# Norms of x turned by a diagonal of reciprocals, and output weights in chunks of 512 by 512

## What is computed

```python
def rmsnorm(x, g):
    xf = x.astype(jnp.float32)
    y = xf * lax.rsqrt(jnp.mean(xf * xf, axis=-1, keepdims=True) + EPS)
    return (y * g.astype(jnp.float32)).astype(x.dtype)
...
        h = rmsnorm(x, norm_mix_g[l])
...
        x = x + merged @ w_o[l]

        h = rmsnorm(x, norm_ffn_g[l])
...
        h = rms_norm(x, norm_mix[i]) * (1 + scale1) + shift1
...
    return o.reshape(B, S, MLA_HEADS * MLA_V) @ w_o
...
        x = x + gate1 * y
        h = rms_norm(x, norm_mlp[i]) * (1 + scale2) + shift2
```

## Time and profile before

| | us |
|---|---|
| median of 3 runs | 1577.72 |
| lowest and highest | 1576.03 and 1578.23 |
| the profiled execution | 1578.04 |
| its span | 1576.2 |
| PE busy | 1530.2 |
| DVE busy | 1151.1 |
| ACT busy | 820.7 |
| POOL busy | 132.2 |

### The profile page before, as it was taken

One profiled execution on the slowest core, in us unless ns is written; L12 is line 12 of the kernel. 1 busy time (PEld: TensorE's weight loads), 2 busy tenths in 40 slices (PEclk: granted clock), 3 DMA queues, 4 the chain that ended last, 5 costly groups with the idle time before them and its releaser, 6 DMA issues. The chain is left out here.

```text
span 1576.2 us, 25674 instructions
## 1 busy us (share of the span) xinstructions
PE 1530.2 (97%) x10406; PEld 1359.2 (86%) x10406; DVE 1151.1 (73%) x1501; ACT 820.7 (52%) x1113; POOL 132.2 (8%) x119
## 2 busy tenths in 40 slices
PE   7999999999999999999998899999999999999998
PEld 6999989999799998999987688887788888878887
DVE  6898678785778767778579667777878766776665
ACT  6464444444646444444478654454556555554442
POOL 2150000000114000000014000000111112000000
PEclk9999999999999999999999999999999999999999
DMA  9766366666676636667632347667886765346652
GB/s 327 266 216 204 131 231 230 212 238 243 234 268 210 209 117 234 207 215 277 235 126 86 101 143 278 243 226 210 266 310 234 269 169 197 108 144 217 207 172 102
DMA packets 229908, 327.45 MB, mean 208 GB/s; under 512 B 12216, under 2 KB 187808, under 8 KB 229792
## 3 DMA queue, kind: packets, MB, share of 16 engines
q1 hardware_dynamic: 222728, 315.11, 59.4%
q10 hardware_dynamic: 7064, 10.71, 1.9%
HBM read 316.32 MB, written 9.47 MB: 207 GB/s over the span
## 5 line engine op out<-in xcount | busy, mean ns | idle before, releaser
L1751 DVE TENSOR_TENSOR wparts<-raw,wparts 128x2048 fp32r<-128x2048 f32 (+1 forms) x240 | 545.6, 2279 | 211.4 <-ACT wparts L1263 211.1
L1263 ACT ACTIVATE wparts<-raw 128x2048 fp32r<-128x2048 f32 (+1 forms) x240 | 454.8, 1898 | 127.8 <-PE bank L563 92.8
L561 PE MATMUL bank<-hT,wparts 128*128 128x256 f32 x1216 | 348.7, 287 | 2.2 <-DVE hT L1852 1.5
L562 PE MATMUL bank<-hT,wparts 128*128 128x256 f32 x1216 | 343.9, 283 | 0.0
L563 PE MATMUL bank<-hT,wparts 128*128 128x256 f32 x1216 | 343.9, 283 | 0.0
L561 PEld LDWEIGHTS bank<-hT,wparts 128*128 128x128 f32 x1216 | 233.0, 192 | 6.8 <-issue 5.6
L562 PEld LDWEIGHTS bank<-hT,wparts 128*128 128x128 f32 x1216 | 233.2, 192 | 0.2
L563 PEld LDWEIGHTS bank<-hT,wparts 128*128 128x128 f32 x1216 | 233.1, 192 | 0.0
L561 PE MATMUL bank<-wparts,aT 128*128 128x512 f32 (+2 forms) x568 | 217.8, 383 | 1.8 <-DVE aT L1916 1.3
L561 PE MATMUL bank<-wparts,hT 128*128 128x512 f32 (+2 forms) x592 | 211.5, 357 | 3.4 <-DVE wparts L1751 1.6
L562 PE MATMUL bank<-wparts,aT 128*128 128x512 f32 (+2 forms) x568 | 213.5, 376 | 0.0
(11 more groups left out here) (287 smaller groups left out, 1890.9 us busy)
## 6 DMA issues: line engine op xcount, KB each, us to landing
raw<-in_mlp_w SPq DMA_DIRECT2D x64, 1024.0 KB, 5.5
ada_raw<-in_ada_w SPq DMA_DIRECT2D x96, 512.0 KB, 6.4
raw<-in_w_ffn_in SPq DMA_DIRECT2D x44, 1024.0 KB, 5.6
raw<-in_w_in SPq DMA_DIRECT2D x43, 1024.0 KB, 5.5
raw<-in_dil_w_in SPq DMA_DIRECT2D x64, 512.0 KB, 4.8
raw<-in_w_ffn_out SPq DMA_DIRECT2D x22, 1024.0 KB, 5.1
raw<-in_w_o SPq DMA_DIRECT2D x8, 1024.0 KB, 4.8
biasb<-head_bias ACTq DMA_DIRECT2D x16, 512.0 KB, 6.1
```

What stands on the lines that cost most here:

```text
L561: pe.matmul(dst, held[:, 0, :], streamed[:, 0, :], start=start, stop=False)
L562: pe.matmul(dst, held[:, 0, :], streamed[:, 1, :], start=False, stop=False)
L1263: act.activation(view(whi[c % SPL], c), view(raw[c % RAW], c), ACT.Copy).then_inc(s_hi, 1)
L1751: dve.tensor_tensor(view(wlo[c % SPL], c), view(raw[c % RAW], c), view(whi[c % SPL], c).bitcast(F32), ALU.subtract).then_inc(s_lo, 1)
```

## The change

**Turning.** x is no longer multiplied. DVE multiplies the 128 x 128 identity by a tile's reciprocals, one to a row, into a diagonal (`turning_diagonal`), once for each token tile, and PE multiplies a block of x by it: the product is the block turned and scaled. That is an ordinary fp32 matmul in place of a transpose. `norm_upper` on ACT and `norm_lower` on DVE are gone; the tiles `xn...` of 128 x 2 x 1024 become `turner...` of 128 x 2 x 128. `TURN_EARLY` is as before.

**Chunks.** `w_o` and the latent output weights come as four chunks of 512 rows by 512 columns. `wide_half` takes two chunks for one half of the output columns, with a bank for each token tile: 24 matmuls of 512 columns a chunk. `four_for_weights` gives the ring of weights a fourth bank for the time. DVE adds four times 512 columns, after the second and the fourth chunk, and ACT squares four times 512 columns where it squared 768 and 256 of each tile. In the latent part, chunk 0 waits for pairs 0 to 3 of the heads, chunk 1 for pairs 4 to 7.

```diff
             for c in range(4):
-                chunk(("WO", l, c), kmajor(A["w_o"][l], 256 * c, 256))
+                out_half, half = divmod(c, 2)
+                chunk(("WO", l, c), kmajor(A["w_o"][l][512 * half:512 * half + 512], 512 * out_half, 512))
...
-            def norm(e, xn):
+            def norm(e, turner):
...
-                    return pe.transpose(banks[k][:, P * t:P * t + P], xn[:, t, P * k:P * k + P], ident[:, :])
-
-                pe.wait_ge(s_xn, 2 * e + 1)
+                    return pe.matmul(banks[k][:, P * t:P * t + P], x[:, t, P * k:P * k + P], turner[:, t, :], start=True, stop=True)
+
+                pe.wait_ge(s_turner, 2 * e + 1)
                 for k in TURN_EARLY[e]:
-                    if k == 4:
-                        pe.wait_ge(s_xn2, 2 * e + 1)
                     turn_block(k, 0)
+                pe.wait_ge(s_turner, 2 * e + 2)
...
+                four_for_weights()
                 for c in range(4):
+                    out_half, half = divmod(c, 2)
                     w = weights(("WO", l, c))
-                    if c < 3:
-                        token_major(("WO", l, c), w, 0, 256, hT, 0, DK, first_of=None if c else ("mg", l))
-                        used(("WO", l, c))
-                for t in range(TT):
-                    token_major(("WO", l, 3, t), w, 0, 256, hT, 0, DK, (t,))
-                used(("WO", l, 3), ("WO", l, 3, 1))
-                norm(2 * l + 1, xnf)
+                    wide_half(("WO", l, out_half), ("WO", l, c), w, half, None if out_half else ("mg", l))
+                three_for_weights()
+                norm(2 * l + 1, turnerf)
...
             def wo():
-                for h in range(0, MH, 2):
-                    emptied(pe, ("OT", unitm(h) // 2))
+                four_for_weights()
                 for c in range(4):
+                    out_half, half = divmod(c, 2)
+                    if c < 2:
+                        for pair in range(4 * half, 4 * half + 4):
+                            emptied(pe, ("OT", unitm(0) // 2 + pair))
                     w = weights(("MO", 0, c))
...
+                    wide_half(("MO", 0, out_half), ("MO", 0, c), w, half, a=aT)
+                three_for_weights()
...
-            def norm_lower(ev, xn, t):
+            def turning_diagonal(ev, turner, t):
                 i = RSTD_OF[ev] + t
                 dve.wait_ge(s_rstd, i + 1)
-                dve.tensor_scalar(xn[:, t, 0:512], x[:, t, 0:512], rstd[:, i % 2, 0:1], None, ALU.mult).then_inc(s_xn, 1)
...
+                dve.tensor_scalar(turner[:, t, :], ident[:, :], rstd[:, i % 2, 0:1], None, ALU.mult)\
+                   .then_inc(s_turner, 1)
...
+                for c in range(3):
+                    split_ahead(("WO", l, c))
+                    if c == 0:
+                        continue
+                    half = c - 1
+                    for t in range(TT):
+                        nm = ("WO", l, half, t)
+                        bk = full(dve, nm)
+                        xs = x[:, t, 512 * half:512 * half + 512]
+                        dve.tensor_tensor(xs, xs, bk[:, :], ALU.add).then_inc(drain_sem(nm), 1)
+                        if (half, t) == (1, 0):
+                            norm_mean(2 * l + 1, 0)
+                norm(2 * l + 1, turnerf)
```

More of the change, by code:

```diff
@@ L592, in _, with wide_half @@
             wide_banks = {}
-            def wide_half(name, chunk_name, w, half, first_of=None, between=idle):
+            def wide_half(name, chunk_name, w, half, first_of=None, between=idle, a=hT):
                 at = 4 * half
@@ L962, in _ @@
             mlp(0)
[L965 removed]
+            norm(6, turnerd)
             four_for_weights()
@@ L1819, in norm @@
                     dve.sem_inc(s_ss, 1)
+                if 0 < ev < 7:
+                    turning_diagonal(ev, turner, 0)
                 norm_mean(ev, 1)
-                if ev in (0, 7):
-                    norm_lower(ev, xn, 0)
-                norm_lower(ev, xn, 1)
+                if ev == 0:
+                    dve.wait_ge(s_const, 16)
+                for t in range(1 if 0 < ev < 7 else 0, TT):
+                    turning_diagonal(ev, turner, t)
             hc, lc = [0], [0]
```

143 lines of the change are left out of this document (45 added, 98 removed).

## The result

| | median | lowest to highest | runs | against before |
|---|---|---|---|---|
| before | 1577.94 | 1575.10 to 1581.27 | 19 | |
| after | 1581.56 | 1577.75 to 1585.75 | 19 | 1.0022 (1.0015 to 1.0028) |

What follows compares the result with a forecast made beforehand. PE, busy for 97% of the span, was taken as the bound, with its idle time at the norms and MO. Terms from +1.5 (norm 0) to -2.65 us (MO) summed to -2.5 on 1578.04: 1575.5 us, range 1573.5 to 1578.5.

Steps and rivals of the forecast that it cites:

- The turning product: Turning one block on PE by an fp32 product with the diagonal: 0.24 us at full clock, 0.45 at half.
- The rival of 0.43 at full clock: A turning product costs as much as a 256-wide one: some 20 us slower in all, 1595 us; chance 0.08.
- The diagonal: DVE makes the diagonal in 0.24 us instead of multiplying x, so each norm's second turning starts 0.25 earlier.
- w_o with norms 1 and 3: Two layers' output weights and following norms: wide chunks -0.9 us, norm +0.43 each; together -0.95.
- Norm 0: First norm, turned at half clock with nothing to hide the products: +1.5 us (1.0 to 1.9).
- Norm 2: Products keep PE busier, so the clock holds and the projection starts earlier: -0.55 us; +1.0 if the clock falls.
- MO: Latent attention's output weights: early start -1.5 us, wide matmuls -1.15; together -2.65.
- Norm 5: Norm behind the latent output: wider DVE and ACT work, but no half-clock stretch; -0.75 us (-0.3 to -1.35).
- Norms 6 and 7: Last two norms, clock undecided by the rows; taken to fall as before: +0.9 us.
- one case: In norms 6 and 7 the clock falls for 3.4 us as it did: +0.8 and +1.2 us.
- The other case: In norms 6 and 7 the clock holds: 0.25 us gained in norm 6, nothing in norm 7.
- clock falls everywhere: Rival: norm 2 costs 1.55 us more, norms 6 and 7 1.1 more; 1578.1 us, no change; chance 0.13.

Runs made afterwards that it cites:

- filled067: The changed kernel plus identity products (overwritten, output unchanged) that keep PE busy ahead of norms 0, 6 and 7; 1575.82 us, 0.9984 of before.
- before_again: The kernel before, unchanged, profiled a second time; 1580.36 us in one execution.
- products_only: The kernel before with all norms turned by products with the diagonal, keeping its own 256-column chunks; 1580.75 us, 1.0009 of before.
- before_held: The kernel before plus products of the identity in front of norms 1 to 7, no other change; 1576.22 us, 0.9985 of before.
- held_transposes: The kernel before with the new chunks, seven table loads later and identity products ahead of norms 1 to 7, still turning by transposes; 1571.51 us, 0.9955 of before.
- held_products: The changed kernel, turning by products, with seven table loads later and identity products ahead of norms 1 to 7; 1576.04 us, 0.9982 of before.
- chunks_only: The changed kernel with all eight norms turned by transposes as before, leaving only the 512 by 512 chunks; 1574.26 us, 0.9977 of before.
- latent_held: The kernel before with 512 by 512 chunks for the latent output weights only, table loads later, identity products ahead of norms 1 to 7; 1572.53 us, 0.9967 of before.
- after_again: The changed kernel, unchanged, profiled a second time; 1582.7 us in one execution.

## Why the prediction was wrong, step by step

- **The turning product, 0.24 at full clock and 0.45 at half: right.** 16 blocks are 32 records; in norm 2 they take 4.25 us with the wait for the second diagonal, in filled067's norm 7 0.12 each. At half clock they stand 0.213 apart, 0.43 a product. The rival of 0.43 at full clock is out.
- **The diagonal, 0.24: 0.28 to 0.29.** It comes 0.2 earlier than the multiplied x did.
- **w_o with norms 1 and 3, -0.95: -0.93 at the first projection (2.24 to 1.76, 2.14 to 1.69), and then given back, +0.7 and +1.1.** The term failed, since it stops at the first projection and left out the loads behind SP's wait for the second half of x, for which PE waits 0.6 and 1.7 us in after. That the edit itself made it worse isn't shown. In after and in before_again alike, PE waits from some 5.6 to 5.8 us between issue and ACT's start on; the loads took 6.36, 7.56, 7.06 and 6.67 us in the two profiles of after, and 5.55, 6.30, 5.85 and 6.65 in those of before.
- **Norm 0, +1.5 (1.0 to 1.9): +2.0 at the first projection, +1.8 after 48 more matmuls: right.** Over five profiles with products and no filling ahead of norm 0 it is +1.3 to +1.8 there. The shift of 2.2 by 154 us is not norm 0's alone: in products_only it shrinks from 1.5 to 0.8 on the same way.
- **Norm 2, -0.55 for a clock that holds: -0.55, which is luck.** The products did hold it, here and in the six other profiles that have products and nothing ahead there. But five of six profiles with transposes and nothing ahead hold it too, by a norm of 15.83 us, and products at full clock are 0.1 slower. What I booked as the change's gain was a fall that before's one profile happened to have.
- **MO, -2.65: -2.70**, of which 1.37 by the early start (1.68 to 0.31 behind the last value product) and 1.33 by the wide matmuls (22.99 to 21.66), where 1.5 and 1.15 were forecast; the two misses cancel. It repeated in every kernel that has it; the second chunk was never late.
- **Norm 5, -0.75: -0.4 in this pair of profiles, inside its range.** As in norm 2, the clock's part of it (before 15.86, 15.09 in its second profile, 14.64 in before_held) isn't the change's.
- **Norms 6 and 7, +0.9 by taking one of two: +1.2 and +2.1, the largest miss.** They fell, as one case had it, at +0.8 and +1.2. That case itself was sized too small: I valued before's start in norm 7 at 1395.5 instead of 1394.72, since its next matmuls ran at half clock. But behind the start PE waits for h anyway, so that the half clock cost before nothing (14.71 fallen, 14.70 held). With products it cost 1.5. The other case was off as well: with the clock held the products don't gain 0.25 in norm 6 and lose nothing in norm 7, they lose 0.05 and 0.5 against transposes with the clock held.

In the traces the forecast is 5.7 us off (-2.5 against +3.2): 2.4 in norms 6 and 7, 1.8 in w_o with norms 1 and 3 and the wait behind them, 0.7 up to the end of the first mixer, 0.3 in MO with norm 5, and 0.5 in norm 4 and the mixers' drift. The state that came, a fall in norms 6 and 7 and none in norms 2 and 5, was worth 1576.6 at the prediction's own prices, so that the clock's choice explains 1 us of the miss and the prices the rest.

What the failed steps on the clock share: I compared the changed kernel's likely clock with one profile's clock of before, and added the difference to medians of many executions. The chances followed from that: 'clock falls everywhere' (1578.1) had 0.13 and was still 3.5 us short of the measured time.

The rule of the Trainium skill that speaks against the edit (Perfetto Trace Analysis, section Transposes: do a logical transpose as a transpose, not as a standard matmul) was the better guide: held_transposes against held_products agrees with it, 1571.51 to 1576.04 us. The Trainium skill's other rule (TensorE: Matmul & The Clock Gate, Part 4: PE-mode transpose), by which transposes don't count as busy for the clock as matmuls do, isn't borne out in before_again's norm 2, where transposes are PE's only work and the granted clock is 1.00. The 9 falls in 30 norms against 1 in 35 go the way of that rule, but a product also keeps PE busy twice as long as a transpose, and no run tells the two apart.

What is not settled: why a load takes 5.2 or 7.6 us; what places a fall of the clock, above all in the latent heads, and why transposes meet more of them; how much the w_o chunks are worth. And the parts don't add up: chunks_only's 0.9977 and products_only's 1.0009 make 0.9986, where the whole is 1.0022; the profiles show the same (-4.4 and +3.1 against +3.2), 3.4 of these 4.5 us by 617 us, behind norm 3. Among them are the late loads of the second layer, 1.2 + 0.5 us of wait in after and none in the other two; and norm 5's 0.3 comes only with both halves together. The rest stays open.

The best version by the median is held_transposes, 1571.51 us over 5 runs, 0.9955 of before (its interval overlaps latent_held's): the change's chunks, x multiplied and transposed as before, the tables one pair of chunks later, and TensorE kept busy ahead of the norms.

## What to carry to other kernels

Before work is moved from engines that wait onto the one that is 97% busy, look at who comes last at the step: as long as TensorE waits for the others there, a slower clock or record hides in that wait, and once TensorE comes last, every record counts, twice where its clock has fallen. Profile the kernel before twice, and give no credit for a fall of the clock that only one profile has; the mean granted clock of many executions tells how many falls there are to gain. When an edit moves a semaphore's moment, go through every queue that waits on it, and look at what stands behind the wait.

## What the runs showed that I had not expected

- One program's granted clock falls at other places from profile to profile: before at norms 2, 5, 6 and 7; before_again at 835, 887, 893, late in norm 5 and in norm 6.
- Products that fill PE's idle time ahead of a norm keep the clock at 1.00 there (filled067, held_transposes, held_products), and took 2.5 us from the kernel before by the medians (before_held, 1576.22 against 1578.70 on its chip; the ratio's interval is 0.9975 to 0.9995).
- Products turn up fewer falls than transposes in norms 1 to 5, 1 in 35 against 9 in 30, and yet the kernel is slower.
- A fall ahead of a wait of PE is given back (after_again, 1.96 to 0.29 us), the same fall behind it is not (held_products).
- Apart from the clock, most norms' lengths repeat within some 0.03 us over eighteen profiles, while a 1 MB load takes 5.2 to 7.6 us at one and the same place.
